# Two blocks of a transformer in one kernel: halves of the first slot, narrow level matmuls, GpSimd's gates and a later turn

## The reference, cut to what matters

```python
def swiglu(h, w_in, w_out):                      # F = 2816
    gate, up = jnp.split(h @ w_in, 2, axis=-1)
    return (jax.nn.silu(gate) * up) @ w_out
...
def step(S, inp):                                # HGRN2, chunk by chunk
    b = jnp.cumsum(lb_c, axis=2)
    diff = b[:, :, :, None, :] - b[:, :, None, :, :]
    decay = jnp.where(causal, jnp.exp(...), 0.0)
    scores = jnp.einsum('bhtk,bhtsk,bhsk->bhts', qb, decay, kb)
...
s = qi @ k * scale + cqi - c                     # fox, causal, 16 heads of 64
o = (softmax(s) @ v) * jax.nn.sigmoid(g)
return o @ w_out
...
mod = (jax.nn.silu(c) @ w_ada + b_ada)           # 1024 x 9216
u = rms_norm(h, norm_pre) * (1.0 + scale) + shift
h = h + resid_w * gate * rms_norm(fn(u), norm_post)
```

## Time and profile before

| | us |
|---|---|
| median of 3 runs | 1626.92 (1625.74 to 1628.73) |
| the profiled execution | 1630.87 |
| its span, first to last instruction | 1629.1 |
| TensorE busy | 1590.8 |
| mean granted clock of TensorE | 0.995 of full |
| TensorE's stops: at the start, up to 12.10 | 11.8 |
| at 29.22, first products | 2.94 |
| at 359.10, 377.98, 876.08: starts of ffn stages two and four | 0.37, 0.36, 0.45 |
| at 556.70, 1080.35: starts of ffn stages three and five | 1.69, 0.70 |
| at 712.60, 1179.18, 1233.28: behind late folds | 3.24, 0.60, 4.84 |
| at 832.51: second attention | 1.81 |
| at 1248.37, 1444.63 | 1.06, 1.71 |

### The profile page before, as it was taken

One profiled execution on the slowest core, in us unless ns is written; L12 is line 12 of the kernel. 1 busy time (PEld: TensorE's weight loads), 2 busy tenths in 40 slices (PEclk: granted clock), 3 DMA queues, 4 the chain that ended last, 5 costly groups with the idle time before them and its releaser, 6 DMA issues.

```text
span 1629.1 us, 20897 instructions
## 1 busy us (share of the span) xinstructions
PE 1590.8 (98%) x7517; PEld 1313.4 (81%) x7517; DVE 1152.6 (71%) x1114; ACT 821.4 (50%) x983; POOL 604.7 (37%) x368
## 2 busy tenths in 40 slices
PE   6999999999999999999999999999998999999998
PEld 5888888988888788877877888888886788878887
DVE  5565668777877787857777787688786557875554
ACT  5455563354445544445656444554435576564443
POOL 0000100068993599920008899079991000000000
PEclk9999999999999999999999999999999999999999
DMA  7767753348887688854437888758794444547672
GB/s 249 222 196 220 236 195 114 107 158 261 260 271 249 193 280 260 273 194 158 153 105 218 280 261 266 249 184 274 257 288 139 155 155 156 172 136 232 198 220 87
DMA packets 243133, 337.23 MB, mean 207 GB/s; under 512 B 14792, under 2 KB 180994, under 8 KB 243074
## 3 DMA queue, kind: packets, MB, share of 16 engines
q1 hardware_dynamic: 196256, 281.05, 52.6%
q0 software_dynamic: 10512, 38.54, 7.6%
q10 hardware_dynamic: 36306, 16.86, 4.1%
HBM read 319.62 MB, written 1.05 MB: 197 GB/s over the span
## 4 chain that ended last, share of the span: by engine, by line
PE 70%; POOL 17%; DVE 5%; ACT 3%; DMA 2%; issue 2%; ACTq 0%; SPq 0%; DVEq 0%; POOLq 0%
PE ps L570 20%; PE ps L572 20%; PE ps L571 20%; POOL arena L542 5%; POOL arena L539 4%; POOL arena L544 3%; POOL arena L548 2%; PE ps L616 2%; DVE w_lo L1835 2%; PE ps L850 2%; POOL arena L533 2%; DMA arena<-w_ada_dram 1%; PE ps L624 1%; PE ps L578 1%; ACT w_hi L1300 1%
## 5 line engine op out<-in xcount | busy, mean ns | idle before, releaser
L1835 DVE TENSOR_TENSOR w_lo<-raw,w_hi 128x2048 fp32r<-128x2048 f32 x266 | 683.6, 2581 | 204.5 <-ACT w_hi L1300 204.0
L1300 ACT CAST w_hi<-raw 128x2048 fp32r<-128x2048 f32 x266 | 505.7, 1911 | 308.7 <-PE ps L572 270.7
L570 PE MATMUL ps<-w_hi,actT_hi 128*128 128x512 f32 x1456 | 572.7, 393 | 6.4 <-DVE hidden L1988 2.9
L572 PE MATMUL ps<-w_hi,actT_lo 128*128 128x512 f32 x1456 | 567.6, 390 | 0.0
L571 PE MATMUL ps<-w_lo,actT_hi 128*128 128x512 f32 x1456 | 567.3, 390 | 0.0
L570 PEld LDWEIGHTS ps<-w_hi,actT_hi 128*128 128x128 f32 x1456 | 273.6, 188 | 66.5 <-issue 6.5
L572 PEld LDWEIGHTS ps<-w_hi,actT_lo 128*128 128x128 f32 x1456 | 273.7, 188 | 57.8
L571 PEld LDWEIGHTS ps<-w_lo,actT_hi 128*128 128x128 f32 x1456 | 273.9, 188 | 55.4
L542 POOL TENSOR_TENSOR arena<-arena 128x512 f32<-128x512 f32 x72 | 192.0, 2666 | 5.6
L570 PE MATMUL ps<-w_hi,hT_hi 128*128 128x512 f32 x480 | 189.6, 395 | 1.7 <-DVE hT_lo L1978 1.7
L539 POOL TENSOR_TENSOR arena<-arena,c_silu 128x1024 f32<-128x1024 f32 x72 | 153.1, 2126 | 95.6 <-DVE actT_lo L1863 44.6
(11 more groups left out here) (257 smaller groups left out, 1349.9 us busy)
## 6 DMA issues: line engine op xcount, KB each, us to landing
raw<-ffn_w_in_dram SPq DMA_DIRECT2D x176, 512.0 KB, 4.9
raw<-ffn_w_out_dram SPq DMA_DIRECT2D x88, 512.0 KB, 4.4
arena<-w_ada_dram POOLq DMA_DIRECT2D x72, 512.0 KB, 6.3
raw<-ffn_w_gate_dram SPq DMA_DIRECT2D x44, 512.0 KB, 4.1
raw<-ffn_w_up_dram SPq DMA_DIRECT2D x44, 512.0 KB, 5.1
raw<-ffn_w_down_dram SPq DMA_DIRECT2D x44, 512.0 KB, 4.4
raw<-w_in_dram SPq DMA_DIRECT2D x40, 512.0 KB, 4.6
raw<-hg_w_in_dram SPq DMA_DIRECT2D x32, 512.0 KB, 4.9
```

What stands on the lines that cost most here:

```text
L570: nc.tensor.matmul(to, hi, whi, start=start, stop=False, skip_group_check=True)
L572: return nc.tensor.matmul(to, lo, whi, start=False, stop=stop, skip_group_check=True)
L1300: nc.scalar.copy(w_hi[:, s, :], raw[:, s, :]).then_inc(hi_ready[s], 1)
L1835: nc.vector.tensor_tensor(w_lo[:, s, :], raw[:, s, :], w_hi[:, s, :].bitcast(F32), ALU.subtract)\
```

## The change

1. **First slot in halves.** SP loads slot 0 in four DMAs of 256 KB, and ScalarE and VectorE split its two halves one by one; TensorE's first four matmuls wait for the first half only.
2. **Small transfers by GpSimd.** The 19 small DMAs move from ScalarE's queue to GpSimd's, behind the first stage's `actT_ready`. `zf_loaded` goes into `small_loaded`, `hg_zeroed` into `levels_ready`.
3. **Narrow keys.** For levels of 32 and 64 a head's matmul loads only the keys of one block (32 or 64 columns) and streams only the queries of its partner; results of even and odd heads stand side by side in partitions. VectorE takes them with plain copies.
4. **GpSimd's gates.** Both groups start when the second (fourth) ffn stage has all its activations, and the pause stands at the 22nd unit of a group, not at the 19th.
5. **Second attention.** `turn_p(3)` goes into the middle of `unit(7, 0)`. VectorE multiplies the second half of tile 0's gates by the inverse sums (`gated(1, 0)`) ahead of the copy of the last result, and `split_lo(1)` goes behind `turn_gated(0)`. TensorE's turn of the gates waits for `fx_o` too.

```diff
+                    if st.norm == 0 and half == 0 and isinstance(c, int) and c == 0:
+                        for part, done in ((slice(0, 2), front_loaded), (slice(2, 4), raw_loaded[0])):
+                            nc.sync.dma_start(to[:, part, 0:FC], w_gate[:, part, 0:FC]).then_inc(done, 16)
+                            nc.sync.dma_start(to[:, part, FC:COLS], w_up[:, part, 0:FC]).then_inc(done, 16)
+                        continue
...
@@ block.gpsimd
+            pool.wait_ge(actT_ready, 4)
...
             pool.wait_ge(levels_loaded, 16)
             pool.wait_ge(hT_turned, 2)
...
-            pool.wait_ge(turned, 4 * (by_name["hg_out"].turned + 1))
             pool.wait_ge(c_ready, 1)
...
             for first in (0, half):
-                if first:
-                    pool.wait_ge(turned, 4 * (by_name["fox_out"].turned + 1))
+                pool.wait_ge(actT_ready, 4 * ((7 if first else 3) + 1))
                 ada_load(first)
                 ada_load(first + 1)
                 for n in range(first, first + half):
-                    if n == first + half // 2:
+                    if n == first + half // 2 + ADA_PER:
                         pool.wait_ge(actT_ready, 4 * ((8 if first else 4) + 1))
...
@@ block.tensor, rounded_first
+                    if st.norm == s == t == 0:
+                        pe.wait_ge(front_lo, 1)
+                    else:
+                        pe.wait_ge(lo_ready[s], st.filled[s] + 1)
                     for kk in range(4):
+                        if st.norm == s == t == 0 and kk == 2:
+                            pe.wait_ge(lo_ready[s], st.filled[s] + 1)
...
+                def narrow(n, t, h):
+                    size = LEVELS[n]
+                    beside = P // 2 // size
+                    for block in range(beside):
+                        rows = block * 2 * size + (h % 2) * size
+                        at = block * 2 * size
+                        to = ps[rows:rows + size, level_bank(n, t), (h // 2) * size:(h // 2 + 1) * size]
+                        last = nc.tensor.matmul(to, tile(hg_kT, t, h)[:, at:at + size], tile(hg_Q, t, h)[:, at + size:at + 2 * size],
+                                                start=True, stop=True, skip_group_check=True)
+                    return last
...
-                turn_p(3)
-                unit(7, 0)
+                unit(7, 0, lambda: turn_p(3))
                 weigh(3)
-                unit(7, 1, lambda: turn_tile(by_name["fox_out"], fx_g, 0))
+                def turn_gates():
+                    pe.wait_ge(fx_o, 4)
+                    turn_tile(by_name["fox_out"], fx_g, 0)
+
+                unit(7, 1, turn_gates)
...
@@ block.scalar
+            def front():
+                act.wait_ge(front_loaded, 32)
+                nc.scalar.copy(w_hi[:, 0, 0:SLOT // 2], raw[:, 0, 0:SLOT // 2]).then_inc(front_hi, 1)
+                act.wait_ge(raw_loaded[0], 32)
+                nc.scalar.copy(w_hi[:, 0, SLOT // 2:SLOT], raw[:, 0, SLOT // 2:SLOT]).then_inc(hi_ready[0], 1)
...
@@ block.vector, masked
+                        if h >= 32:
+                            for odd in range(2):
+                                for block in range(P // 2 // h):
+                                    at, rows = 2 * h * block, 2 * h * block + h * odd
+                                    last = nc.vector.tensor_copy(hg_sc[at:at + h, t, odd:HG_H:2, at + h:at + 2 * h],
+                                                                 ps[rows:rows + h, level_bank(n, t), 0:HG_H // 2 * h]
+                                                                 .rearrange("p (g n) -> p g n", g=HG_H // 2))
+                            last.then_inc(hg_masked, 1)
+                            continue
...
@@ block.vector, fox
                 split_lo(0, nxt.filled[0])
+                inverse_sums(3)
+                gated(1, 0).then_inc(src_ready, 1)
+                keep_result(3)
+                dve.wait_ge(fx_o, 4)
+                turn_gated(0)
                 split_lo(1, nxt.filled[1])
-                scaled(3)
-                dve.wait_ge(fx_o, 4)
-                step.wait()
-                for t in range(TILES):
-                    gated(1, t).then_inc(src_ready, 1)
-                    if t == 0:
-                        turn_gated(0)
+                gated(1, 1).then_inc(src_ready, 1)
                 split_lo(2, nxt.filled[2])
                 split_lo(3, nxt.filled[3])
                 turn_gated(1)
```

More of the change, by code:

```diff
@@ L352, in build @@
         hg_turned, hg_q, hg_sig, hg_k = sem("hg_turned"), sem("hg_q"), sem("hg_sig"), sem("hg_k")
[L353 removed]
+        hg_kT_ready, hg_qf = sem("hg_kT_ready"), sem("hg_qf")
         hg_totaled, hg_upd, hg_scored, hg_masked, hg_crossed, hg_copied = (sem(n) for n in (
@@ L522, in _ @@
             nc.gpsimd.memset(eps_col, EPS).then_inc(eps_ready, 1)
+            pool.wait_ge(actT_ready, 4)
+            at = 48
+            for v, n in ((a["norm_pre_2"].rearrange("l i (k p) -> (l i k) p", p=P), 24),
+                         (a["norm_post_2"].rearrange("l i (k p) -> (l i k) p", p=P), 24),
+                         (a["c_2"].rearrange("b (k p) -> (b k) p", p=P), KD),
+                         (a["hg_lb_logits"].rearrange("l (k p) -> (l k) p", p=P), HG_H), (a["hg_out_norm_g"], 1)):
+                nc.gpsimd.dma_start(rows_a[at:at + n, :], v).then_inc(rows_loaded, 16)
+                at += n
+            for v in (a["fox_q_norm_g"], a["fox_k_norm_g"]):
+                for i in range(2):
+                    nc.gpsimd.dma_start(rows_a[at:at + 1, i * FOX_D:(i + 1) * FOX_D], v).then_inc(rows_loaded, 16)
+                at += 1
+            nc.gpsimd.dma_start(rows_a[at:at + 1, :], a["da_subln_2"]).then_inc(rows_loaded, 16)
+            nc.gpsimd.dma_start(rows_b[0:72, :], a["b_ada_2"].rearrange("l (k p) -> (l k) p", p=P)).then_inc(rows_loaded, 16)
+            nc.gpsimd.dma_start(fox_b, a["fox_b_f"]).then_inc(small_loaded, 16)
+            for i, v in enumerate(("q1", "k1", "q2", "k2")):
+                nc.gpsimd.dma_start(lam_row[:, DA_D * i:DA_D * (i + 1)], a[f"da_lambda_{v}_2"]).then_inc(small_loaded, 16)
+            nc.gpsimd.dma_start(zf_raw[:, :, :], tiled(a["fox_w_in"][0])[:, :, 4 * D:FOX_IN]).then_inc(small_loaded, 16)
+            nc.gpsimd.dma_start(consts[:, P:], a["consts"][:, P:]).then_inc(consts_loaded, 16)
+            nc.gpsimd.dma_start(levels_raw, a["levels"]).then_inc(levels_loaded, 16)
             pool.wait_ge(levels_loaded, 16)
@@ L846, in score @@
                                 rhs = tile(hg_qT, t, h)
+                            elif LEVELS[n] >= 32:
+                                last = narrow(n, t, h)
+                                continue
                             else:
@@ L1387, in after_out @@
                     for b in range(2):
-                        if t == 0:
+                        if t == b == 0 and st is None:
+                            front()
+                        elif t == 0:
                             split_hi(b, nxt.filled[b])
@@ L1790, in _ @@
             after_out(None, stages[0])
[L1792 to L1804, removed]
-            nc.scalar.dma_start(fox_b, a["fox_b_f"]).then_inc(small_loaded, 16)
-            for i, v in enumerate(("q1", "k1", "q2", "k2")):
-                nc.scalar.dma_start(lam_row[:, DA_D * i:DA_D * (i + 1)], a[f"da_lambda_{v}_2"]).then_inc(small_loaded, 16)
-            nc.scalar.dma_start(zf_raw[:, :, :], tiled(a["fox_w_in"][0])[:, :, 4 * D:FOX_IN]).then_inc(zf_loaded, 16)
-            nc.scalar.dma_start(consts[:, P:], a["consts"][:, P:]).then_inc(consts_loaded, 16)
-            nc.scalar.dma_start(levels_raw, a["levels"]).then_inc(levels_loaded, 16)
             for st in stages:
@@ L1836, in split_lo, with front @@
                     .then_inc(lo_ready[s], 1)
+            def front():
+                for at, hi, lo in ((slice(0, SLOT // 2), front_hi, front_lo), (slice(SLOT // 2, SLOT), hi_ready[0], lo_ready[0])):
+                    dve.wait_ge(hi, 1)
+                    nc.vector.tensor_tensor(w_lo[:, 0, at], raw[:, 0, at], w_hi[:, 0, at].bitcast(F32), ALU.subtract)\
+                        .then_inc(lo, 1)
             def turn(st, b):
@@ L1952, in after_out @@
                 norm(nxt, 0)
-                split_lo(0, nxt.filled[0])
+                if st is None:
+                    front()
+                else:
+                    split_lo(0, nxt.filled[0])
                 turn(nxt, 0)
```

28 lines of the change are left out of this document (16 added, 12 removed).

## The result

The changed kernel takes 1641.63 us (median of 4 runs, 1640.67 to 1642.93) against 1626.72 (1625.74 to 1628.73): 1.009 times, 95% interval 1.0073 to 1.0107. It is slower by 0.9%; forecast was 1622.1, 0.3% faster. The profiled execution took 1640.67, 9.8 more than the one of before; the medians differ by 14.9.

The account below looks back on a forecast made before the run. TensorE was taken as the bound (busy 1590.8 of 1629.1 us). Front -5.2, narrow keys -3.4, second attention -1.8 and gates +5.6 sum to -4.8: 1626.1 profiled, 1622.1 at the median; range 1612 to 1632, the forecast's own 1617 to 1626.

Parts of the forecast that it names:

- Front: Start of the kernel: slot 0 in halves and small transfers on GpSimd together gain 5.2 us, bounds 2.9 and 6.5.
- the 1.1 of the halves: First slot: TensorE starts 2.15 us earlier but then stands for slot 1; gain 1.1, bounds 0.3 and 2.15.
- Narrow keys: Levels 32 and 64: TensorE's 7.0 us become 3.0, 0.6 lost waiting for VectorE; gain 3.4, bounds 0 and 4.0.
- Rival C: Small gains hidden, no change: column groups don't overlap (0 to 1 of 3.4), other gains shrink; 1626.0 us, chance 0.28.
- Second attention: TensorE no longer stands 1.81 us at `turn_p(3)` for the last exponentials; gain 1.8, bounds 0 and 2.0.
- Gates, the gains: Ends of ffn stages 3 and 5 lose stops and half clock, 12.2 us; starts of stages 2 and 4 gain 1.2.
- 3.95 off for the median: The earlier profiled execution (1630.87 us) lay 3.95 above the median, so this was subtracted from the summed forecast.
- Gates, the costs: Late GpSimd units stop TensorE in ffn stages 2 and 4, 17.0 us (bounds 0 and 27), plus 2.0 at boundaries.
- 8.5 a stage, 2.0 for the boundaries: Ffn stages 2 and 4: 7.1 us of stops plus 1.4 of half clock each; norms beside GpSimd 1.0 per boundary.
- a free allowance of its own, 5.6 and 4.9: VectorE's fold waits up to 5.6 us in chunk 6 and 4.9 in chunk 9 were taken not to stop TensorE.
- A: Rival: waiting VectorE frees GpSimd only half as much (7.9 a unit), stages 2 and 4 starve; 1632.1 us, chance 0.13.
- B: Rival: GpSimd keeps up (units at most 8.3 us), no fold costs TensorE anything; 1605.1 us, chance 0.11.

Follow-up runs that it names:

- gates_back: The changed kernel with both GpSimd gates (group start and pause) as before; 1617.41 us, 0.9936 times the kernel before.
- pause_back: The changed kernel with only GpSimd's pause back at unit 18, the late group start kept; 1636.49 us, 1.0055 times the kernel before.

## Why the prediction was wrong

**Front: right in this execution, in part by luck.** -5.3 (8.82 less the 3.54 of the narrow keys) against -5.2. First weight matmul at 10.14, a stop of 1.44 at 15.37, none near 29. It is one of the four profiled executions of nine without half clock behind that stop, which takes 1.7 to 2.0. The small transfers gave 4.4 in their trace for the 4.1 that I took; the 1.1 of the halves is not borne out.
```profile
10.14 0.80 PE L647 MATMUL ps<-w_hi,actT_hi 128*128 128x512 f32 x1 [0.82 <-ACT actT_hi L1368]
...
15.37 0.47 PE L647 MATMUL ps<-w_hi,actT_hi 128*128 128x512 f32 x1 [1.44 <-DVE w_lo L1873]
```
**Narrow keys: right in sum.** -3.5 against -3.4. The matmuls are cheaper than I had them (level 32: twice 0.46 for 32 records; behind the second 32 the next matmul starts 0.39 after the first of them, 0.012 each where I took 0.026; level 64: 1.15; together 2.1 for 3.0) and the wait for VectorE's update dearer, 1.00 for 0.6. That is 3.9; where the other 0.4 went isn't placed. Rival C had 0 to 1 here, and is wrong. Whether it is the smaller load or the column groups side by side that makes them cheap was not taken apart.
```profile
293.09 0.46 PE L870 MATMUL ps<-arena 128*32 128x32 f32 x32
294.55 0.46 PE L870 MATMUL ps<-arena 128*32 128x32 f32 x32 [1.00 <-DVE arena L2120]
```
**Second attention: right.** No stop at `turn_p(3)` or `turn_gates`; from 804.17 to 876.08 it took 71.9, in gates_back 793.25 to 863.38, 70.1, with like stops at the end: -1.8.

**Gates, the gains: right against the profiled execution, some 5 too large for the median.** Ends of stages 3 and 5: 3.24 + 0.60 + 4.84 idle and 3.8 of half clock gone, 12.5 for 12.2; starts of stages 2 and 4 some 1.0 for 1.2. But I took 3.95 off for the median and at the same time counted stage 3's 4.8 as a gain, which most likely were that 3.95. The same time was counted twice.

**Gates, the costs: wrong, 32.8 for 19.0.** The term "8.5 a stage, 2.0 for the boundaries" failed:

| | forecast | stage 2 | stage 4 |
|---|---|---|---|
| fold waits, chunks 3, 6, 9 | 4.7, 8.8, 8.8 | 6.23, 8.43, 6.22 | 6.23, 8.42, 6.22 |
| stop, chunk 3 | 0 | 0.95 | 0.72 |
| stop, chunk 6 | 3.2 | 5.29 | 6.24 |
| stop, chunk 9 | 3.9 | 4.00 | 4.00 |
| half clock behind stops | 1.4 | 4.1 | 3.1 |
| boundary | 1.0 | 1.94 | 2.43 |
| sum | 9.5 | 16.3 | 16.5 |

The waits were forecast well in sum (22.3 in all, 20.9 measured), not one by one: chunk 3's is 1.5 longer, chunk 9's 2.6 shorter. Chunk 5's fold waited 1.19 and 0.35 besides, which I had at nothing. Three steps behind them failed. First, I gave each fold a free allowance of its own, 5.6 and 4.9, read from stages that waited once or twice. What was free in chunk 6 is VectorE's lead at that time, and chunk 3's wait had spent it: 3.1 and 2.2 in place of 5.6, so 2.5 and 3.4 a stage. In chunk 3 the stop of 0.95 and 0.72 is for the most part the longer wait. Second, half clock: I charged it once a stage, but there are two stops of 4 or more, and each cost 1.5 to 2.5. Third, I moved the pause for the stage it frees, and priced the three units that it moves into the end of the stage before at the norms alone (1.0); they also slow VectorE on its way from the last fold to the last `hidden`, 2.8 and 2.4 (pause_back). That chunk 9's stop came out as forecast is chance: a wait shorter by 2.6 and a slower way behind it cancel.

Net of the gates: 32.8 - 12.5 - 1.0 = +19.3, with the other parts (-5.3 - 3.5 - 1.8) +8.7; the profiled executions differ by 9.8. Of the other 1.1, some 0.5 are scattered slower starts of matmuls in stage 2; the rest isn't placed.

**The rivals.** What happened is A's outcome: GpSimd starves stages 2 and 4, at 14.3 and 14.1 (boundaries apart) for its 13.5. Its 1632.1 fell short by the boundaries (4.4 for 2.0), these 1.4, and the 5 of the median. But it didn't come by A's condition. A waiting VectorE frees GpSimd fully: then a unit takes 6.24 from issue to issue, near the 6.5 of the forecast and far from A's 7.9. B is refuted by the waits. I let the chance of A (0.13) hang on one number, the pace, where the allowance, the clock and the boundary each led to the same end; and the range's upper bound rested on A's 13.5 instead of adding the bounds of these.

## What to carry to other kernels

- Free slack between two engines is a stock, not an allowance for each wait: read the lead in the trace ahead of each wait, and ask what spends it and what refills it (a stop of the consumer does). Then price the producer's way behind the wait too: with the same lead of 5.2 it left 5.0 free in one kernel and 2.2 in the other. One read in a stage with one wait is an upper bound.
- When a helper engine's work is moved, price both ends: the same later pause was a gain of 5.8 with the early start and cost 6 a stage with the late one. And where the profiled execution lies off the median, ask which stop makes it so before selling that stop.

## What the runs showed of the hardware

Most fold waits take one of a few values, the same in all kernels: 0.35, 1.17, 2.54, 4.51, 6.22, 8.4. The timeline around the wait of 8.43 (from 457.34) shows why; VectorE, then GpSimd:
```profile
453.77 3.56 DVE L1873 TENSOR_TENSOR w_lo<-raw,w_hi 128x2048 fp32r<-128x2048 f32 x1 [0.25 <-ACT w_hi L1349]
```
```profile
453.27 1.91 POOL L566 TENSOR_TENSOR arena<-arena,c_silu 128x1024 f32<-128x1024 f32 x1
455.26 3.24 POOL L569 TENSOR_TENSOR arena<-arena 128x512 f32<-128x512 f32 x1
458.58 0.74 POOL L571 TENSOR_TENSOR arena<-arena 128x256 f32<-128x256 f32 x1
459.39 0.46 POOL L575 TENSOR_TENSOR arena<-arena 128x128 f32<-128x128 f32 x1
460.15 0.92 POOL L560 DMA_DIRECT2D arena<-w_ada_dram  x1 [0.30 <-POOL arena L575]
...
466.39 0.92 POOL L560 DMA_DIRECT2D arena<-w_ada_dram  x1 [0.66 <-POOL arena L575]
```
VectorE's subtraction (2.28 alone) ends 2.2 after L566, and L569 (1.29 alone) ends 1.2 after that subtraction: they take turns, a whole instruction at a time. When VectorE falls idle, GpSimd stands just at the start of an operation, so the wait is the sum of whole operations that are left of the unit. The Trainium skill ("SBUF — State Buffer", section "Who interferes with whom") calls it an exclusive lock, and these rows agree. It works both ways, which I had counted for the norms alone: beside GpSimd VectorE's L1873 took 3.35 for 2.28 and L1914 1.89 for 0.76.

Matmuls whose weights fill 32 of 128 columns, with 32 moving columns and in neighbouring column groups, cost a small part of the full-width ones. Behind the 32 records at 294.55 the next matmul starts at 294.94, 0.39 later, 0.012 each; behind the 64 full-width ones with 64 moving columns, at 294.77, it starts 7.06 later, 0.110 each.
